# A decoder layer in fp32: the input projection in three passes over its rows in place of two, and heads four steps apart

## Chip, cores and metric

The kernel runs on one core of one Trainium2 chip. The metric is the device time of one execution in microseconds (us): the median of the runs.

## What is computed

```python
m = silu(c) @ w_mod + b_mod                     # 2048 -> 6 x 2048: sh1, sc1, g1, sh2, sc2, g2
hm = rms_norm(x) * (1 + sc1) + sh1              # x: 256 x 2048
q, k, v, o, g = split(hm @ w_in)                # 8 heads, q and k 128 wide, v and o 256 wide
y = (sigmoid(o) * rms_norm(mlstm(q, k, v, g)) * h_norm) @ w_out
x = x + g1 * y
hf = rms_norm(x) * (1 + sc2) + sh2
u = causal_conv3(hf @ w_up) + conv_b            # w_up: 2048 x 11264
x = x + g2 * ((silu(gate(u)) * val(u)) @ w_down)
```

All of it is fp32. Each product is computed as three products of fp32r parts (a rounded high part and the rest): high by high, high by low, low by high.

## The kernel before

**Shared stream of weights.** Weights come in as *halves* of 512 KB (`load_half` for `w_in`). For each half, ScalarE rounds it to `w_hi` (`split_hi`), VectorE subtracts to get `w_lo` (`split_lo`), and TensorE multiplies it (`in_half`, then `b_half`). `raw` holds eight halves, `w_hi` and `w_lo` four each. Step `p` of ScalarE and VectorE handles half `p + 3`, and ScalarE begins it when TensorE has finished `p` halves (`slot_hi`). So step `p` of these two engines lies beside TensorE's half `p`.

**Passes and strips.** The projection `hm @ w_in` needs scale and shift for the rows of `hm` that it multiplies. To begin before all of them are there, it is done in passes over the 16 row tiles (128 rows each). A pass goes through 12 *strips* of 512 columns (4 of V, 4 of O, 2 of K, 2 of Q), two row tiles a half. The first pass takes row tiles 0 to 5, the second 6 to 15. Between the passes a strip's sums are stored from PSUM to SBUF by ScalarE, and put back into PSUM (seeded) later. Strips of V and O take 12 matmuls of 512 columns a half, strips of K and Q 24 of 256.

**Scale and shift.** `m` is a vector: `w_mod` is read row tile by row tile. `load_m0` brings columns 0 to 767 of both chunks (scale, then shift) in 16 loads of two row tiles. VectorE adds three of four row tiles, scaled by `c`, to `acc` (`add_m0`), and TensorE sums the fourth and then the column sums of `acc` (`sum_m0`, `column_sums`). Columns 768 to 2047 follow during pass 1 (`load_m1`, `add_m1`, 32 loads of one row tile). The four other chunks are added in the same way later (`load_mod`, `add_mod`, 2048 columns at a time, called *accumulations* here), at steps that the table `MOD_SLOT` gives. Loads of the queue SP are issued in one order, written out by hand.

**Heads.** In the last pass V and O strips come last, and the eight heads of the mLSTM are worked off between the halves, in `attend(e)`, where `e` counts halves from the first V strip of that pass. TensorE's part of `attend(e)` stands behind half `e`; VectorE's part stands in step `e`, behind `split_lo` and ahead of the accumulation of that step. Head `h` has its scores behind half 5 + 5h (`E_SCORES`), its product with V behind 9 + 5h (`E_PV`), the gated output `gated` on VectorE in step 12 + 5h (`E_PV + 3`), and the transposes of `gated` behind half 13 + 5h (`E_HT`); `E_HEAD = 5` is the distance of two heads. TensorE runs its instructions in order, so the transposes, and every half behind them, wait for `gated`:

```python
h = head_at(e, E_HT)
if h is not None:
    pe.wait_ge(gated_made, 2 * h + 2)
```

Of the kernel before, what the change touches and what calls it, by code (L numbers as in the profile page):

```python
# [5 lines left out]
def hybrid_mlstm_convffn_adaln_kernel(nc, x_d, c_d, w_mod, b_mod, w_in, gate_bias, h_norm, w_out,  # L6
# [27 lines left out]
    K_FIRST = 6  # L34
    PAIRS = (K_FIRST // 2, (KT - K_FIRST) // 2)
    PASS = ([("V", j) for j in range(4)] + [("O", j) for j in range(4)]
            + [("K", 0), ("K", 1), ("Q", 0), ("Q", 1)],
            [("K", 0), ("K", 1), ("Q", 0), ("Q", 1)]
            + [(kind, j) for j in range(4) for kind in "VO"])
    STRIPS = len(PASS[0])  # L40
    V_PASS1 = STRIPS * PAIRS[0]
    V_VO = V_PASS1 + 4 * PAIRS[1]
    V_OUT = V_PASS1 + STRIPS * PAIRS[1]
# [5 lines left out]
    for n in CHUNKS:  # L49
# [13 lines left out]
    M0_COLS, M1_COLS = K_FIRST * P, (KT - K_FIRST) * P  # L63
    MODS_ALONE = 2 * KT


    MOD_SLOT = [V_PASS1 + p for p in (5, 7, 8, 10, 12, 13, 15, 17, 18)] \
        + [V_VO + e for e in (0, 1, 3, 4, 6, 8, 9, 11, 13, 14, 16, 18, 19, 21, 23, 24, 26, 28, 29, 31, 33, 34,
                              36, 38)] \
        + [V_OUT + f for f in (2, 4, 5, 7, 9, 10, 12, 13, 15, 17, 19, 21, 23, 26, 28)]  # L70
# [5 lines left out]
    MOD_LOAD = [V_PASS1 + 5, V_PASS1 + 6] + [max(V_PASS1 + 6, p + 11) for p in MOD_SLOT[:MOD_WIDE]] \  # L76
# [3 lines left out]
    E_SCORES, E_PV, E_HT, E_HEAD = 5, 9, 13, 5  # L80
    E_GATE = 18

    with ExitStack() as ctx:
# [12 lines left out]
        m0 = place("m0", [P, 8, 2 * M0_COLS], 0)  # L96
        m1 = place("m1", [P, 3, M1_COLS], 32 * KB)
# [95 lines left out]
        evac0, seeded, evac1 = sem("evac0"), sem("seeded"), sem("evac1")  # L193
# [112 lines left out]
        def _(sp):  # L306
# [24 lines left out]
            def load_m0(i):  # L331
                n, rows = i // 8, 2 * (i % 8) * P
                if i >= 8:
                    wait_m0(i - 8)
                sp.dma_start(m0[:, i % 8, :].rearrange("p (j n) -> p j n", j=2),
                             w_mod[rows:rows + 2 * P, MOD_ORDER[n]:MOD_ORDER[n] + M0_COLS]
                             .rearrange("(j p) n -> p j n", p=P)).then_inc(m0_in[i % 8], 16)

            def load_m1(i):
                n, rows = i // KT, (i % KT) * P  # L340
                if i < 3:
                    wait_m0((14, 14, 15)[i])
                else:
                    sp.wait_ge(m1_used, i - 2)
                col = MOD_ORDER[n] + M0_COLS
                sp.dma_start(m1[:, i % 3, :], w_mod[rows:rows + P, col:col + M1_COLS])\
                  .then_inc(m1_in[i % 3], 16)

            def load_half(vh):
# [29 lines left out]
            for vh in range(6):  # L379
                load_half(vh)  # L380
            for i in range(2 * KT):
                load_m1(i)
                load_half(6 + i)
            for vh in range(6 + 2 * KT, V_OUT):
# [59 lines left out]
        def _(pool):  # L444
# [83 lines left out]
            pool.wait_ge(colsum_done, 5)  # L528
# [20 lines left out]
        def _(act):  # L549
# [87 lines left out]
            def store_strip(m):  # L637
                for b in range(2):
                    nc.scalar.activation(strip_sums(0, m)[b], bank_pair(m, b), ACT.Copy)\
                             .then_inc(evac0, 1)  # L640

            def seed_strip(m):

                if m == STRIPS:
                    act.wait_ge(evac0, 2 * (STRIPS - 1))
                elif m == STRIPS + 1:
                    act.wait_ge(evac0, 2 * STRIPS)
                else:
                    act.wait_ge(evac1, 2 * (m - 1 - STRIPS))
                for b in range(2):  # L650
                    nc.scalar.activation(bank_pair(m, b), strip_sums(1, m)[b], ACT.Copy)\
                             .then_inc(seeded, 1)
# [897 lines left out]
```

## Time and profile before

| | |
|---|---|
| time, median of 3 runs | 1219.88 us (1215.63 to 1220.29) |
| span of the profiled execution | 1212.4 us |
| TensorE (PE) busy | 1187.3 us, 98% of the span |
| VectorE (DVE) busy | 922.2 us, 76% |
| ScalarE (ACT) busy | 623.4 us, 51% |
| bytes moved | 313.55 MB, mean 259 GB/s |

The profile gives its execution only by its span, from the first to the last instruction; it gives no time of its own for it. The runs lie 3.2 to 7.9 us above that span. What is worked out below is a difference of spans, and is taken off the median as it is.

How to read the rows: PE is TensorE's matmuls, PEld its weight loads, SPq the queue that issues the loads. PEclk is the granted clock of TensorE, where 1.00 is 2.4 GHz and 0.50 is 1.2 GHz. A busy PE is modelled to each matmul's end, so counts of matmuls in a stage say more than its share.

### The profile page before, as it was taken

How to read it: one execution, taken by the hardware profiler on the slowest of the kernel's cores; microseconds unless marked ns; L12 is line 12 of the kernel's file. 1: busy time of each engine (PE TensorE's matmuls, PEld its weight loads, DVE VectorE, ACT ScalarE, POOL GpSimd, SP SyncE). 2: the span in 40 equal slices, each digit the busy share in tenths (PEclk: the TensorE clock that was granted, in tenths of full speed). 3: DMA queues.
4: the chain of work that ended last, by engine and by line, in shares of the span. 5: the costliest groups of instructions: out<-in, count | busy, mean ns of one | idle time of the engine just before them, and what ended most of it. 6: DMA issues, size and time to landing. Idle time of an engine off the chain costs nothing.

```text
span 1212.4 us, 18009 instructions
## 1 busy us (share of the span) xinstructions
PE 1187.3 (98%) x6338; PEld 1020.6 (84%) x6338; DVE 922.2 (76%) x1016; ACT 623.4 (51%) x888; POOL 147.0 (12%) x158
## 2 busy tenths in 40 slices
PE   5899999999999999999999999999999999999998
PEld 5788999877788888888888888888888888888887
DVE  5899878788897897998887446888885446777654
ACT  4354564655554456565554445555554545555442
POOL 0000110001111120221121000212211000221100
PEclk9699999999999998999999999999999999999999
DMA  9999989798989994898885568878865566676542
GB/s 361 369 397 401 395 283 392 295 373 306 327 311 346 387 308 137 243 260 227 232 251 207 180 208 241 229 210 256 231 210 203 181 204 177 189 191 176 203 160 85
DMA packets 260028, 313.55 MB, mean 259 GB/s; under 512 B 6056, under 2 KB 186728, under 8 KB 251272
## 3 DMA queue, kind: packets, MB, share of 16 engines
q1 hardware_dynamic: 259360, 312.51, 78.0%
q8 instruction: 32, 0.52, 0.2%
q10 hardware_dynamic: 442, 0.21, 0.1%
q0 software_dynamic: 176, 0.16, 0.1%
q14 instruction: 18, 0.15, 0.0%
HBM read 310.76 MB, written 2.10 MB: 258 GB/s over the span
## 4 chain that ended last, share of the span: by engine, by line
PE 84%; DMA 8%; DVE 4%; issue 1%; SPq 1%; ACT 1%; DVEq 0%; ACTq 0%
PE ps L1203 27%; PE ps L1204 14%; PE ps L1231 9%; PE ps L1232 9%; PE ps L1233 9%; DMA m<-in_l_w_mod_dram 7%; PE ps L1280 2%; PE ps L1282 2%; PE ps L1281 2%; PE ps L1290 2%; PE ps L1293 2%; PE ps L1292 2%; DVE acc L905 1%; DVE acc L932 1%; PE ps L1301 1%
## 5 line engine op out<-in xcount | busy, mean ns | idle before, releaser
L892 DVE TENSOR_TENSOR w_lo<-raw,w_hi 128x1024 fp32r<-128x1024 f32 x392 | 481.9, 1231 | 197.8 <-ACT w_hi L559 197.1
L559 ACT ACTIVATE w_hi<-raw 128x1024 fp32r<-128x1024 f32 x392 | 414.1, 1057 | 357.9 <-PE ps L1233 167.7
L1203 PE MATMUL ps<-hm,w_hi 128*128 128x512 f32 x1408 | 495.9, 398 | 0.0
L1204 PE MATMUL ps<-hm,w_lo 128*128 128x256 f32 x1408 | 394.2, 280 | 0.0
L1203 PEld LDWEIGHTS ps<-hm,w_hi 128*128 128x128 f32 x1408 | 265.1, 188 | 65.5 <-issue 0.3
L1204 PEld LDWEIGHTS ps<-hm,w_lo 128*128 128x128 f32 x1408 | 266.1, 189 | 0.1
L1231 PE MATMUL ps<-w_hi,act_hi 128*128 128x512 f32 x344 | 134.3, 390 | 0.0
L1233 PE MATMUL ps<-w_hi,act_lo 128*128 128x512 f32 x344 | 133.9, 389 | 0.0
L1232 PE MATMUL ps<-w_lo,act_hi 128*128 128x512 f32 x344 | 133.9, 389 | 0.0
L1280 PE MATMUL ps<-w_hi,hm 128*128 128x512 f32 x256 | 103.6, 405 | 2.7 <-DVE hm L943 2.7
L1282 PE MATMUL ps<-w_hi,hm 128*128 128x512 f32 x256 | 100.4, 392 | 0.0
L539 POOL TENSOR_TENSOR act_full<-conv_gate,conv_val 128x256 f32<-128x256 f32 x44 | 32.5, 738 | 558.9 <-DVE conv_val L1173 558.9
L1281 PE MATMUL ps<-w_lo,hm 128*128 128x512 f32 x256 | 100.2, 391 | 0.0
L905 DVE SCALAR_TENSOR_TENSOR acc<-mod_raw,cT,acc 128x2048 f32<-128x2048 f32 x40 | 94.7, 2368 | 2.6 <-DMA mod_raw<-in_l_w_mod_dram 1.6
L853 ACT ACTIVATE up_sum<-ps 128x256 f32<-128x256 f32 x88 | 33.5, 380 | 106.5 <-PE ps L1204 106.5
L1231 PEld LDWEIGHTS ps<-w_hi,act_hi 128*128 128x128 f32 x344 | 64.6, 188 | 13.7 <-issue 0.2
L1233 PEld LDWEIGHTS ps<-w_hi,act_lo 128*128 128x128 f32 x344 | 64.6, 188 | 13.5
L1232 PEld LDWEIGHTS ps<-w_lo,act_hi 128*128 128x128 f32 x344 | 64.6, 188 | 13.4 <-issue 0.2
L1290 PE MATMUL ps<-hm,w_hi 128*128 128x256 f32 x256 | 73.3, 286 | 0.0
L1293 PE MATMUL ps<-hm,w_lo 128*128 128x256 f32 x256 | 73.2, 286 | 0.0
L1292 PE MATMUL ps<-hm,w_hi 128*128 128x256 f32 x256 | 73.1, 286 | 0.0
L543 POOL TENSOR_TENSOR act_lo<-act_full,act_hi 128x256 f32 x44 | 65.1, 1479 | 23.7 <-DVE act_hi L1180 23.7
(181 smaller groups left out, 1377.8 us busy)
## 6 DMA issues: line engine op xcount, KB each, us to landing
raw<-in_l_w_up_dram SPq DMA_DIRECT2D x88, 1024.0 KB, 5.9
mod_raw<-in_l_w_mod_dram SPq DMA_DIRECT2D x56, 1024.0 KB, 6.5
raw<-in_l_w_in_dram SPq DMA_DIRECT2D x96, 512.0 KB, 8.1
raw<-in_l_w_down_dram SPq DMA_DIRECT2D x44, 1024.0 KB, 5.0
m<-in_l_w_mod_dram SPq DMA_DIRECT2D x32, 640.0 KB, 7.2
raw<-in_l_w_out_dram SPq DMA_DIRECT2D x16, 1024.0 KB, 8.5
m<-in_l_w_mod_dram SPq DMA_DIRECT2D x16, 768.0 KB, 13.5
mod_wide<-in_l_w_mod_dram SPq DMA_DIRECT2D x8, 1024.0 KB, 7.2
```

Source lines behind the costliest of these rows:

```text
L559: nc.scalar.activation(w_hi[:, v % 4, :], raw[:, v // 2 % 4, (v % 2) * HALF:(v % 2 + 1) * HALF], ACT.Copy).then_inc(w_hi_made, 1)
L892: nc.vector.tensor_tensor(w_lo[:, v % 4, :], raw[:, v // 2 % 4, (v % 2) * HALF:(v % 2 + 1) * HALF], w_hi[:, v % 4, :].bitcast(f32), ALU.su ...
L905: nc.vector.scalar_tensor_tensor(out=part, in0=src, scalar=cT[:, ds(tile, 1)], in1=part, op0=ALU.mult, op1=ALU.add).then_inc(mod_done, 1)
L1203: mm(ps[:, 4 + w % 4, :], hi, both, start=(k == 0), stop=False, skip_group_check=True)
L1204: return mm(ps[:, 4 + w % 4, 0:SEQ], lo, hm_hi[:, k, :], start=False, stop=(k == KT - 1), skip_group_check=True)
L1231: mm(out, s_hi, hi, start=first, stop=False, skip_group_check=True)
L1232: mm(out, s_hi, lo, start=False, stop=False, skip_group_check=True)
L1233: last = mm(out, s_lo, hi, start=False, stop=final, skip_group_check=True)
L1280: mm(out, s_hi, hi, start=(k == 0), stop=False, skip_group_check=True)
L1281: mm(out, s_hi, lo, start=False, stop=False, skip_group_check=True)
L1282: last = mm(out, s_lo, hi, start=False, stop=(k == final), skip_group_check=True)
L1290: mm(out, hi, hm_hi[:, k, :], start=(k == 0 and f % 2 == 0), stop=False, skip_group_check=True)
```

## The change

- Three passes over row tiles: 0 to 3, 4 to 7, 8 to 15. Twelve strips more are stored and seeded.
- `load_m0` brings 512 columns of scale and shift, in 16 loads of 512 KB that have 16 buffers of their own.
- The other columns come in two groups: 512 columns in 16 loads of two row tiles for pass 2, and 1024 columns in 32 loads of one row tile for pass 3. They are added at steps 0 to 15 (two a step) and 16 to 43.
- The last pass has four halves a strip in place of five: 16 halves of K and Q and 32 of V and O, where there were 20 and 40. The number of halves in all stays 96.
- The heads stand four halves apart. `E_PV + 3` is still 12, and `E_HT` is now 12. The table of accumulations is new: ten in the K and Q steps (nine before), 21 in the 32 V and O steps (24 in 40), 17 behind them (15).

```diff
-    K_FIRST = 6
-    PAIRS = (K_FIRST // 2, (KT - K_FIRST) // 2)
+    K_AT = (0, 4, 8, KT)
+    LAST = len(K_AT) - 2
+    PAIRS = [(K_AT[n + 1] - K_AT[n]) // 2 for n in range(LAST + 1)]
...
-    MOD_SLOT = [V_PASS1 + p for p in (5, 7, 8, 10, 12, 13, 15, 17, 18)] \
...
+    M_TILES = (2, 1)
+    M_LOADS = [2 * KT // r for r in M_TILES]
+    M_FIRST = [0, M_LOADS[0]]
+    M_ADDS = [(n, i, j) for n in range(2) for i in range(M_LOADS[n]) for j in range(M_TILES[n])]
+    ADD_SLOT = [a // 2 for a in range(2 * KT)] + [KT + a * 28 // (2 * KT) for a in range(2 * KT)]
+    LOAD_HALF = [4 + i for i in range(M_LOADS[0])] + [4 + KT + i * 27 // (2 * KT) for i in range(M_LOADS[1])]
...
+    MOD_SLOT = [V_LAST + p for p in (3, 4, 6, 7, 8, 10, 11, 12, 14, 15)] \
+        + [V_VO + e for e in (0, 1, 3, 4, 6, 7, 9, 10, 12, 13, 15, 17, 18, 19, 21, 23, 24, 25, 27, 29, 30)] \
+        + [V_OUT + f for f in (1, 2, 3, 5, 6, 8, 9, 10, 11, 13, 15, 17, 19, 21, 23, 26, 28)]
...
-    E_SCORES, E_PV, E_HT, E_HEAD = 5, 9, 13, 5
-    E_GATE = 18
+    E_SCORES, E_PV, E_HT, E_HEAD = 5, 9, 12, 4
+    E_GATE = 16
...
-        m0 = place("m0", [P, 8, 2 * M0_COLS], 0)
-        m1 = place("m1", [P, 3, M1_COLS], 32 * KB)
+        m0 = place("m0", [P, 16, 2 * M0_COLS], 16 * KB)
+        m1 = place("m1", [P, 4, KB], 32 * KB)
...
-            for p in range(V_PASS1):
+            for p in range(V_VO):
                 in_half(p)
-                if p == 24:
-                    pe.wait_ge(m1_used, KT)
-                    pe.wait_ge(sc_made, 2)
-                    column_sums(0, SUM_BANK[0], K_FIRST, KT)
-                if p == V_PASS1 - 3:
-                    pe.wait_ge(m1_used, 2 * KT)
-                    column_sums(1, SUM_BANK[1], K_FIRST, KT)
-            for p in range(V_PASS1, V_VO):
-                in_half(p)
+                for n in range(1, LAST + 1):
+                    for chunk in range(2):
+                        if p == V_AT[n] - (9, 3)[chunk]:
+                            pe.wait_ge(m1_used, 2 * KT * (n - 1) + KT * (chunk + 1))
+                            pe.wait_ge(sc_made, 2 * n)
+                            column_sums(chunk, SUM_BANK[chunk], K_AT[n], K_AT[n + 1])
```

The change moves instructions at three places. The first is TensorE ahead of the first half: the sum of the last load and the column sums of the shift chunk. Before:

```order
L1337 MATMUL ps<-cT,m_51 128x1 [waits m0_in6]
L1337 MATMUL ps<-cT,m_51 128x1 x5
L1301 MATMUL ps<-ones,acc 128x1 [waits m0_used]
L1301 MATMUL ps<-ones,acc 128x1 x5
L1280 MATMUL ps<-w_hi,hm 128x512 [waits raw_done,hm_made]
```

and now:

```order
L1348 MATMUL ps<-cT,m_51 128x1 [waits m0_in14]
L1348 MATMUL ps<-cT,m_51 128x1 x3
L1312 MATMUL ps<-ones,acc 128x1 [waits m0_used]
L1312 MATMUL ps<-ones,acc 128x1 x3
L1291 MATMUL ps<-w_hi,hm 128x512 [waits raw_done,hm_made]
```

Six column tiles became four at each step, and the loads have semaphores (`m0_in`) of their own.

The second is VectorE at the head of pass 1, where `m_52` is the buffer of the later columns and `w_lo` is the split of a half. Before:

```order
L939 TENSOR_SCALAR hm_full<-hm_full,scale_p,shift_p 128x256
L943 TENSOR_TENSOR hm<-hm_full,hm 128x256
L892 TENSOR_TENSOR w_lo<-raw,w_hi 128x1024 x2
L932 SCALAR_TENSOR_TENSOR acc<-m_52,cT,acc 128x1280
L892 TENSOR_TENSOR w_lo<-raw,w_hi 128x1024
L932 SCALAR_TENSOR_TENSOR acc<-m_52,cT,acc 128x1280
```

and now:

```order
L964 TENSOR_TENSOR hm<-hm_full,hm 128x256
L897 TENSOR_TENSOR w_lo<-raw,w_hi 128x1024 x2
L939 SCALAR_TENSOR_TENSOR acc<-m_52,cT,acc 128x512 x2
L897 TENSOR_TENSOR w_lo<-raw,w_hi 128x1024
L939 SCALAR_TENSOR_TENSOR acc<-m_52,cT,acc 128x512 x2
L897 TENSOR_TENSOR w_lo<-raw,w_hi 128x1024
```

One addition of 1280 columns a step became two of 512; from step 16 on it is one of 1024 in most steps.

The third is VectorE at the heads, behind the first V strip of the last pass: the accumulation `acc<-mod_raw` ends a step, and `gated` is what TensorE's transposes wait for. One head before:

```order
L905 SCALAR_TENSOR_TENSOR acc<-mod_raw,cT,acc 128x2048
L892 TENSOR_TENSOR w_lo<-raw,w_hi 128x1024
L1021 SCALAR_TENSOR_TENSOR probs<-ps,weights 128x384
L1042 SCALAR_TENSOR_TENSOR gated<-ps,small,o_sig 128x256 x2
L892 TENSOR_TENSOR w_lo<-raw,w_hi 128x1024
L905 SCALAR_TENSOR_TENSOR acc<-mod_raw,cT,acc 128x2048
L892 TENSOR_TENSOR w_lo<-raw,w_hi 128x1024
L1002 TENSOR_SCALAR m_sel<-m_row,ident 8x256
```

and a head now:

```order
L910 SCALAR_TENSOR_TENSOR acc<-mod_raw,cT,acc 128x2048
L897 TENSOR_TENSOR w_lo<-raw,w_hi 128x1024
L1032 SCALAR_TENSOR_TENSOR probs<-ps,weights 128x384
L910 SCALAR_TENSOR_TENSOR acc<-mod_raw,cT,acc 128x2048
L897 TENSOR_TENSOR w_lo<-raw,w_hi 128x1024
L1013 TENSOR_SCALAR m_sel<-m_row,ident 8x256
L1053 SCALAR_TENSOR_TENSOR gated<-ps,small,o_sig 128x256 x2
L897 TENSOR_TENSOR w_lo<-raw,w_hi 128x1024
```

`gated` moved from the step of `probs` to the next one. It stands behind one accumulation, one split and `m_sel` more. On TensorE the transposes stand one half nearer to the product with V: behind the half that lies beside the step of `gated`, where before they stood behind the half after it.

## Rows read from the trace of the kernel before

**Rows 1.** The page: span, and busy time of each engine.

```profile
span 1212.4 us, 18009 instructions
...
PE 1187.3 (98%) x6338; PEld 1020.6 (84%) x6338; DVE 922.2 (76%) x1016; ACT 623.4 (51%) x888; POOL 147.0 (12%) x158
```

**Rows 2.** Busy time by stage; last columns: granted clock, DMA share, GB/s.

```profile
core 0: us, PE busy (x) PEld busy (x) DVE busy (x) ACT busy (x) POOL busy (x), PEclk, DMA share, GB/s
28.00:41.86 13.86, 12.14 (x58) 11.97 (x58) 10.18 (x11) 0.00 (x0) 0.00 (x0) 0.52 1.03 399
...
60.00:100.00 40.00, 40.00 (x178) 33.15 (x177) 37.79 (x29) 20.07 (x25) 0.00 (x0) 1.00 1.03 398
147.66:158.00 10.34, 10.34 (x75) 10.34 (x76) 7.06 (x11) 4.99 (x10) 3.49 (x3) 0.83 0.96 342
176.00:214.80 38.80, 38.80 (x325) 38.80 (x325) 33.80 (x22) 17.81 (x21) 0.00 (x0) 1.00 0.97 369
265.00:339.20 74.20, 73.17 (x335) 58.26 (x336) 65.65 (x83) 41.62 (x71) 10.41 (x16) 1.00 0.89 318
```

**Rows 3.** Timeline up to the first projection matmul: start, length, engine, line.

```profile
41.86 2.07 DVE L923 SCALAR_TENSOR_TENSOR acc<-m,cT,acc 128x768 f32<-128x768 f32 x2 [0.74 <-DMA m<-in_l_w_mod_dram]
...
43.99 2.72 PE L1301 MATMUL ps<-ones,acc 128*128 128x1 f32 x12 [1.36 <-DVE acc L923]
...
44.57 1.06 ACT L559 ACTIVATE w_hi<-raw 128x1024 fp32r<-128x1024 f32 x1 [0.30 <-DMA raw<-in_l_w_in_dram]
...
46.95 2.08 ACT L597 ACTIVATE hm<-hm_full,shift_p,scale_p 128x256 fp32r<-128x256 f32 x4
...
49.40 0.80 PE L1280 MATMUL ps<-w_hi,hm 128*128 128x512 f32 x1 [2.69 <-DVE hm L943]
```

**Rows 4.** Waits, TensorE alone: total us, times, longest.

```profile
PE ps L1393 <- DVE gated L1042: 1.1, 2, 0.7
PE ps L1301 <- DVE acc L932: 0.3, 1, 0.3
```

**Rows 5.** The page's DMA issues: KB each, median us to landing.

```profile
mod_raw<-in_l_w_mod_dram SPq DMA_DIRECT2D x56, 1024.0 KB, 6.5
...
m<-in_l_w_mod_dram SPq DMA_DIRECT2D x16, 768.0 KB, 13.5
```

**Rows 6.** Timeline, TensorE, the later column sums of the shift chunk.

```profile
147.66 2.39 PE L1301 MATMUL ps<-ones,acc 128*128 128x1 f32 x20 [0.28 <-DVE acc L932]
```

**Rows 7.** Lines from 49.4 to 214.8 us: count, busy us, mean ns.

```profile
L892 DVE TENSOR_TENSOR w_lo<-raw,w_hi 128x1024 fp32r<-128x1024 f32 x56 | 68.4, 1221 | 8.9 <-ACT w_hi L559 8.6
...
L932 DVE SCALAR_TENSOR_TENSOR acc<-m,cT,acc 128x1280 f32<-128x1280 f32 x32 | 49.6, 1550 | 6.3 <-DMA m<-in_l_w_mod_dram 6.0
```

**Rows 8.** Timeline of one head on TensorE, VectorE and ScalarE (others left out).

```profile
320.76 0.60 PE L1393 MATMUL ps<-ident,gated 128*128 128x128 f32 x4
...
324.60 0.33 DVE L1002 TENSOR_SCALAR m_sel<-m_row,ident 8x256 f32<-8x256 f32 x1
...
333.60 2.34 DVE L905 SCALAR_TENSOR_TENSOR acc<-mod_raw,cT,acc 128x2048 f32<-128x2048 f32 x1
...
333.75 0.39 PE L1280 MATMUL ps<-w_hi,hm 128*128 128x512 f32 x1
...
335.86 1.22 DVE L892 TENSOR_TENSOR w_lo<-raw,w_hi 128x1024 fp32r<-128x1024 f32 x1
...
336.47 0.39 PE L1280 MATMUL ps<-w_hi,hm 128*128 128x512 f32 x1
...
336.67 1.06 ACT L559 ACTIVATE w_hi<-raw 128x1024 fp32r<-128x1024 f32 x1 [1.48 <-PE ps L1282]
...
336.99 0.55 DVE L1021 SCALAR_TENSOR_TENSOR probs<-ps,weights 128x384 f32<-128x384 f32 x1
...
337.46 0.86 DVE L1042 SCALAR_TENSOR_TENSOR gated<-ps,small,o_sig 128x256 f32<-128x256 f32 x2
...
338.24 1.21 DVE L892 TENSOR_TENSOR w_lo<-raw,w_hi 128x1024 fp32r<-128x1024 f32 x1
```

More of the change, by code:

```diff
@@ L183, in hybrid_mlstm_convffn_adaln_kernel @@
         pool_step = sem("pool_step")
-        m0_in = [sem(f"m0_in{s}") for s in range(8)]
+        m0_in = [sem(f"m0_in{s}") for s in range(16)]
         m0_used, m0_summed = sem("m0_used"), sem("m0_summed")
-        m1_in = [sem(f"m1_in{s}") for s in range(3)]
+        m1_in = [sem(f"m1_in{s}") for s in range(4)]
         m1_used = sem("m1_used")
@@ L192, in hybrid_mlstm_convffn_adaln_kernel @@
         half_done = sem("half_done")
-        evac0, seeded, evac1 = sem("evac0"), sem("seeded"), sem("evac1")
+        stored, seeded = sem("stored"), sem("seeded")
         mod_in = [sem(f"mod_in{s}") for s in range(2)]
@@ L378, in _ @@
                 load_m0(i)
[L379 to L384, printed above, removed]
+            for vh in range(V_OUT):
+                for i in range(len(LOAD_HALF)):
+                    if LOAD_HALF[i] == vh:
+                        load_m1(i)
                 load_due_mods(vh)
@@ L635, in scale_shift, with seed_strip @@
                     nc.scalar.activation(out, src, ACT.Copy).then_inc(sc_made, 1)
-            def store_strip(m):
+            def seed_strip(m):
+                act.wait_ge(stored, 2 * (m - 1))
                 for b in range(2):
[L639 to L651, printed above, removed]
+                    nc.scalar.activation(bank_pair(m, b), strip_sums(m)[b], ACT.Copy)\
                              .then_inc(seeded, 1)
@@ L957, in _ @@
             dve.wait_ge(sc_made, 2)
-            dve.wait_ge(xT_copied, K_FIRST // 2)
-            for g in range(K_FIRST // 2):
+            dve.wait_ge(xT_copied, K_AT[1] // 2)
+            for g in range(K_AT[1] // 2):
                 modulate_lo(0, 2 * g, 2 * g + 2)
@@ L1260, in in_half @@
                 bank = strip_banks(m)
-                first, final = (0, 2 * PAIRS[0] - 1) if n == 0 else (2 * PAIRS[0], KT - 1)
+                first, final = K_AT[n], K_AT[n + 1] - 1
                 if 2 * kp == first and m >= 2:
                     if n == 0:
-                        pe.wait_ge(evac0, 2 * (m - 1))
+                        pe.wait_ge(stored, 2 * (m - 1))
                     else:
@@ L1334, in sum_m0 @@
                 n, rt = i // 8, 2 * (i % 8)
-                pe.wait_ge(m0_in[i % 8], 16 * (n + 1))
-                for k in range(K_FIRST):
-                    last = mm(ps[:, SUM_BANK[n], k:k + 1], m0[:, i % 8, k * P:(k + 1) * P],
+                pe.wait_ge(m0_in[i], 16)
+                for k in range(K_AT[1]):
+                    last = mm(ps[:, SUM_BANK[n], k:k + 1], m0[:, i, k * P:(k + 1) * P],
                               cT[:, rt:rt + 1], start=(rt == 0 and k == 0), stop=False,
@@ L1416, in attend @@
                     if h == 0:
-                        pe.wait_ge(evac1, 8)
+                        pe.wait_ge(stored, taken(4))
                         pe.wait_ge(aem_made, 1)
```

205 lines of the change are left out of this document (104 added, 101 removed).

## Prediction

> **What bounds the kernel now.** I read the page first: TensorE is busy for 98% of the span, VectorE for 76%, ScalarE for 51% [rows 1]. So the question is where TensorE waits, and what stands ahead of its first half. The waits of TensorE alone answer the first part: behind the start there are only 1.1 us for `gated` at two heads and 0.3 us for an addition ahead of the column sums [rows 4]. The timeline of the start answers the second. The last load of scale and shift is added from 41.86 us, the column sums end at 46.7, and the first half begins at 49.40 [rows 3]. In the stages until then the DMA engines are full, at 399 GB/s [rows 2]: the start is a matter of bytes, all that comes behind it of TensorE's instructions. The change leaves the projection's matmuls as they are. A V or O half lasts 2.70 us (178 matmuls in 40 us, 12 a half), a K or Q half 2.87 (325 in 38.8 us, 24 a half) [rows 2].
>
> **The start.** The 16 first loads shrink from 768 KB [rows 5] to 512 KB: 16 x 0.262 MB = 4.19 MB less, at 399 GB/s 10.5 us. Behind the last load two additions get shorter. One of 768 columns takes 1.03 us [rows 3], one of 1280 takes 1.55 [rows 7], so 1.0 ns a column, and 0.77 us at 512: 0.5 us less for two. The column sums are 8 records in place of 12, 2.72 / 12 each [rows 3]: 0.9 us less. Not all of this 1.4 us counts. The splits of the first two halves hang on loads that land behind the last of scale and shift, and ScalarE's second one ends at 45.63, 1.3 us ahead of the modulation at 46.95 [rows 3]; VectorE's splits follow. I take 0.8. The first half begins 11.3 us earlier. Bounds: TensorE also does 32 transposes and the sums of the loads ahead of this; with loads coming every 1.3 us in place of 2, I take at worst 1.5 us of that as backlog, so 9.8. At best the first halves no longer meet the half clock that the start leaves behind (0.50 to 0.52 until 49.4 [rows 2]); the first matmul takes 0.80 us where later ones take 0.39 [rows 3, 8], and some 3 us at half rate give 1.5 back: 12.8.
>
> The Trainium skill, "DMA: Bandwidth & Descriptors", section "Bandwidth", advises transfers of 1 MiB and more, and its section "Anatomy of one DMA — SWDGE (gpsimd) path" fits, for loads that GpSimd issues, 2.0 us + bytes / 436 GB/s to one of them. By that fit smaller pieces save less: 16 x 0.262 MB / 436 GB/s = 9.6 us, an estimate, and the fixed part stays. The trace agrees only in part: halves of 512 KB and pieces of 640 KB together move at 398 GB/s from 60 to 100 us [rows 2], so nothing of a fixed part shows where they queue.
>
> **Passes 1 and 2.** Twelve strips more are stored and seeded, four copies each on ScalarE, which is busy for half of the time [rows 1]; TensorE has two bank pairs, and a strip of two halves (5.4 us) covers split, store and seed. I cost it at nothing; were a strip late, it would show as a wait for `seeded`. VectorE has 1.22 + 2 x 0.77 = 2.76 us a step where it had 1.22 + 1.55 = 2.77 [rows 7]: the same. The DMA queue carries 48 pieces and 43 halves of 0.524 MB in 43 steps, 1.11 MB or 2.77 us a step at 400 GB/s; before it was 1.18 MB, 2.95 us, with 0.3 us of wait at its end [rows 4]. So nothing is added.
>
> Column sums: 24 tiles in place of 20, at 2.39 us for ten [rows 6], so 1.0 us more. But they are now four pieces of 1 to 1.9 us. Behind the old piece of 2.39 us the clock was granted at 0.83 over 10.3 us [rows 2, 6], worth 1.8 us. If shorter pieces leave it alone, the sum is 1.0 - 1.8 = -0.8 us. If the two of 1.9 us do what the one did, it is +2.8.
>
> **K and Q steps of the last pass.** Sixteen halves and ten accumulations of 1.05 MB are 18.9 MB, 47 us at 400 GB/s, against 16 x 2.87 = 45.9 us; before, 20 halves and nine made 19.9 MB in 57.4 us. An accumulation needs its buffer back: landing takes 6.5 us [rows 5] and the addition 2.3 [rows 8], with two buffers one in 4.4 us, and the table asks for one in 3.8. VectorE falls behind by 9 x 0.6 = 5 us at most. It works three halves (8.6 us) ahead, so I take 0, and 5 us as the upper bound.
>
> **The heads.** This is the price. `gated` and the transposes behind the same half now have one step between them less. Put T for the start of half 12 + 4h. ScalarE begins its split 0.20 us after a half starts (336.67 against 336.47) and takes 1.06; then VectorE's split 1.13 (335.86 to 336.99), `m_sel` 0.26 and `gated` 0.78 (337.46 to 338.24) [rows 8]. That ends at T + 3.43, while the half has ended at T + 2.72: TensorE waits 0.71 us in every head, even when VectorE is idle ahead of it. (`m_sel` is 0.33 long; 0.26 is from its start to the next one's.)
>
> Where the step before has an accumulation, the chain is longer. From the start of that step: 0.20 + 1.06 + 1.13, `probs` 0.47, the accumulation 2.26 (333.60 to 335.86), then 1.13 + 0.26 + 0.78, in all 7.29 us, against two halves of 2.72 [rows 8]: a wait of 1.85 us. A second look gives the same: the old head has `gated` done at 338.24, and its transposes due one half after 336.47, at 339.19, so 0.95 us early. One half less, and `m_sel` ahead of it, makes 2.0 us late. The table has an accumulation in steps 15, 19, 23, 27 and 35, and none in 11, 31 and 39. So five heads wait 1.85 and three 0.71: 11.4 us. What TensorE lost there before, 1.1 us [rows 4], goes off: +10.3. Queued behind the transposes is all of TensorE's stream, so nothing gives it back. Bounds: eight times the floor, 5.7 - 1.1 = 4.6; and above, 2.3 us a head if landings make accumulations late besides, 18.4 - 1.1 = 17.3.
>
> Is VectorE itself full? It was busy for 65.65 of 74.2 us over four heads, 16.4 a head, with five splits and three accumulations [rows 2]. With four and 2.6 it is 16.4 - 1.2 - 0.9 = 14.3, against 18.5 - 2.7 = 15.8 for TensorE. So it is the order, not the load.
>
> **Sum.** -11.3 - 0.8 + 0 + 10.3 = -1.8 us, on the profiled span of 1212.4 [rows 1] and so on the median: 1219.9 - 1.8 = 1218.
>
> **Rivals.**
> - *The heads wait less than I think (faster).* If accumulations don't delay `gated`, only the floor is left: -11.3 - 0.8 + 4.6 = -7.5, 1212 us. For it: VectorE has 1.5 us a head to spare. Against: the split, the accumulation and `gated` stand in one queue in this order. 0.2.
> - *The clock falls at the heads (slower).* Until now TensorE keeps 1.00 over the heads, with waits of 0.7 us [rows 2, 4]; it fell behind 0.28 us of wait and 2.39 us of column sums [rows 2, 6]. A wait of 1.85 us with transposes behind it comes near that. Each fall costs about 1.5 us, five of them 7.5: 1226. It decides from four falls on. 0.15.
> - *Late accumulations in the K and Q steps, and on into the first heads (slower).* Up to 5 us there and some 3 at the heads: 1226. For it: the queue is asked for 18.9 MB in the time of 18.4. 0.13.
> - *The change doesn't bring its start.* The bytes of scale and shift are the same in all, only later. If the queue were the bound up to the last piece, TensorE would wait there. Before, the column sums at 147.66 waited for the last addition of 1.55 us [rows 6, 7], so the last piece was there at 146 us. Ten halves more are due by the new last piece, 5.2 MB or 13 us: 159 us, where TensorE comes to its column sums at 38.1 + 1.5 + 124 + 2 = 166. Seven us are to spare; used up, they would cost about as much again, 1224. 0.07.
> - What I forecast: 0.45.
>
> The Trainium skill, "TensorE: Matmul & The Clock Gate", section "HAM oscillation — how this bites in real kernels", says that pauses between bursts of matmuls can put the array back to half rate, and that each one is then paid again. By that rule the heads would come out as in the second rival, 1226. In the trace so far the pauses of the heads leave the clock at 1.00 [rows 2, 4]; no row has one of 1.85 us.
>
> **How the numbers follow.** A measurement of this kernel tells about 0.5% (6 us) from no change. The forecast's own range adds its bounds in part: 1218 - 3 to 1218 + 5. The range reaches down to the first rival with the best start (1.5 us more), 1210, and up to the slow rivals with 3 us of the heads' upper bound, 1229. Faster than 1213.8: the first rival for the most part, and the forecast with a better start, 0.22. Slower than 1226: more than half of the slow rivals, and the forecast with the heads' upper bound, 0.26. Same: 0.52.
>
> **What the changed profile would show.** The first half at about 38.1 us; TensorE's waits with a line for `gated`, eight times, 11 us in all, of 0.7 and 1.9 us; column sums without a wait for additions; granted clock 1.00 over the heads. I am wrong if the waits for `gated` sum to under 6 us or over 16, if the clock falls there, or if waits for `raw_done` or `seeded` (splits of VectorE, seeds of ScalarE) show in passes 2 and 3.

## The result and the profile after

The changed kernel takes 1233.39 us (median of 4 runs, 1229.18 to 1236.14), the kernel before 1219.85 beside it: a ratio of 1.012, 95% interval 1.0098 to 1.0141. It is slower by 13.5 us where I forecast 1.8 us less, and outside my range. The profiled span went from 1212.4 to 1230.2 us, by 17.8. (A run of the changed kernel lies 1.8 us over its own span, 1232.01 against 1230.2; the profiled execution of before was one of its shorter ones.) One of the runs reported below, of e5, took 6658 us and is left out of the ratios.

The page of the changed kernel, as in [rows 1]:

```profile
span 1230.2 us, 18084 instructions
...
PE 1184.0 (96%) x6306; PEld 1015.1 (83%) x6306; DVE 931.1 (76%) x1048; ACT 650.1 (53%) x938; POOL 155.6 (13%) x158
```

TensorE's busy share fell from 98 to 96%. Its waits answer to [rows 4]: engine and line, what it waited for, us in all, times, longest. Those of the start are left out.

```profile
PE ps L1401 <- DVE gated L1053: 14.3, 8, 3.4
...
PE ps L1392 <- ACT em_row L732: 3.3, 1, 3.3
...
PE ps L1291 <- ACT ps L654: 3.0, 2, 1.8
...
PE ps L1301 <- ACT ps L654: 2.1, 1, 2.1
```

L1393 of before is L1401 now. Before, 1.4 us were waited behind the start; now it is 22.9, of which 0.2 for `hm` are not shown and the rest is in three groups. The first line is the heads. The second is `em_row`, a row of gate values that TensorE transposes at `e` = 3, ahead of the first head. The last two are matmuls that wait for a *seeded* bank pair (L654 is `seed_strip`, L1291 and L1301 are the first matmul of a V or O and of a K or Q strip). `gated` I had in the sum, `em_row` only in a rival, and the seeds at nothing.

Where the time goes by milestones, in us from the start of the span, read from TensorE's timeline:

| kernel | first half | K, Q of last pass from | V, O from | output projection from | column sums of chunk 3 |
|---|---|---|---|---|---|
| before | 49.4 | – | 220.5 | 362.7 | 400.0 |
| after | 38.7 | 185.6 | 237.3 | 371.4 | 417.7 |

Chunk 3, counted from 0 in `MOD_ORDER`, is `sc2`, and its column sums stand in the output projection. Behind them both kernels take the same, 812.4 and 812.5 us, so all of the 17.8 us lies ahead. From the first half to there the changed kernel takes 28.4 us longer (379.0 against 350.6): 21.5 more of waits (22.9 - 1.4), 1.0 of four more column tiles, about 4.4 of half clock (5.9 against 1.5, worked out below), and some 1.5 that no row names.

### The profile page after: what moved, and what is told of

The parts are those of the page before. It is cut to its first block, busy times and chain, and to the rows that moved or that the text cites. A ratio compares the mean times of both kernels' runs of the same rounds, so it can differ in the third digit from the quotient of the medians.

```text
span 1230.2 us, 18084 instructions
## 1 busy us (share of the span) xinstructions
PE 1184.0 (96%) x6306; PEld 1015.1 (83%) x6306; DVE 931.1 (76%) x1048; ACT 650.1 (53%) x938; POOL 155.6 (13%) x158
## 4 chain that ended last, share of the span: by engine, by line
PE 78%; DMA 8%; DVE 7%; issue 2%; ACT 2%; SPq 2%; POOL 1%; DVEq 0%; ACTq 0%; POOLq 0%
PE ps L1214 26%; PE ps L1215 13%; PE ps L1243 8%; PE ps L1242 8%; PE ps L1244 8%; DMA mod_raw<-in_l_w_mod_dram 5%; DMA raw<-in_l_w_in_dram 3%; PE ps L1291 2%; DVE acc L910 2%; PE ps L1292 2%; PE ps L1293 2%; SPq L347 2%; DVE w_lo L897 1%; ACT w_hi L572 1%; DVE acc L939 1%
## 5 line engine op out<-in xcount | busy, mean ns | idle before, releaser
L1291 PE MATMUL ps<-w_hi,hm 128*128 128x512 f32 x256 | 105.2, 411 | 6.2 <-DVE hm L964 3.2
L910 DVE SCALAR_TENSOR_TENSOR acc<-mod_raw,cT,acc 128x2048 f32<-128x2048 f32 x40 | 94.9, 2371 | 13.3 <-DMA mod_raw<-in_l_w_mod_dram 10.2
L1293 PE MATMUL ps<-w_hi,hm 128*128 128x512 f32 x256 | 101.4, 396 | 0.0
L1243 PEld LDWEIGHTS ps<-w_lo,act_hi 128*128 128x128 f32 x344 | 64.6, 188 | 13.5 <-issue 0.2
L1301 PE MATMUL ps<-hm,w_hi 128*128 128x256 f32 x256 | 72.8, 285 | 2.3 <-ACT ps L654 2.1
```

The lines of the kernel that those rows point to most:

```text
L910: nc.vector.scalar_tensor_tensor(out=part, in0=src, scalar=cT[:, ds(tile, 1)], in1=part, op0=ALU.mult, op1=ALU.add).then_inc(mod_done, 1)
L1243: mm(out, s_hi, lo, start=False, stop=False, skip_group_check=True)
L1291: mm(out, s_hi, hi, start=(k == 0), stop=False, skip_group_check=True)
L1293: last = mm(out, s_lo, hi, start=False, stop=(k == final), skip_group_check=True)
L1301: mm(out, hi, hm_hi[:, k, :], start=(k == 0 and f % 2 == 0), stop=False, skip_group_check=True)
```

## Experiments

Eleven kernels, each an edit of the changed kernel, timed against the kernel before. Ratios have their 95% interval. The last column is the milestone of above, where TensorE comes to the column sums of chunk 3: 400.0 us before and 417.7 in the changed kernel.

| run | median us | ratio | span | waits for `gated`, us, times | column sums at |
|---|---|---|---|---|---|
| e1 | 1228.1 | 1.0084 (1.0053 to 1.0115) | 1226.7 | 8.3, 6 | 411.0 |
| e2 | 1235.85 | 1.0149 (1.0117 to 1.0181) | 1234.9 | 15.2, 8 | 419.3 |
| e3 | 1225.33 | 1.0067 (1.0042 to 1.0092) | 1218.3 | 6.6, 8 | 407.1 |
| e4 | 1235.25 | 1.0155 (1.0121 to 1.0189) | 1228.6 | 13.3, 8 | 415.7 |
| e5 | 1220.46 | 1.003 (1.0009 to 1.0051) | 1219.4 | 3.5, 5 | 402.0 |
| e6 | 1228.21 | 1.0095 (1.0069 to 1.0122) | 1225.1 | 15.4, 8 | 412.5 |
| e7 | 1230.87 | 1.0121 (1.0085 to 1.0157) | 1226.3 | 14.2, 8 | 413.8 |
| e8 | 1218.82 | 0.9999 (0.9982 to 1.0015) | 1218.2 | 5.5, 5 | 402.1 |
| e9 | 1210.23 | 0.9933 (0.9914 to 0.9953) | 1207.3 | 5.8, 6 | 394.4 |
| e10 | 1214.27 | 0.9975 (0.9957 to 0.9993) | 1210.8 | 4.5, 5 | 398.1 |
| e11 | 1236.42 | 1.0136 (1.0111 to 1.0161) | 1235.8 | 15.0, 8 | 419.7 |

The spans need care. Behind the milestone the edits move nothing but a few accumulations, and yet five kernels take 815.6 to 817.4 us there (e1, e2, e5, e8, e11) and the others 811.2 to 812.9. From 80 to 200 us behind it, TensorE issues 339 to 342 matmuls in 60 us in the five and 345 to 348 in the others, at a granted clock of 1.00 in all. No run shows why. So what an edit does to the passes and the heads is read at the milestone, and a span carries up to 6 us of something else.

### The heads: e1 and e3

e1 puts `gated` at the head of its step:

```diff
+                gate_head(p - V_VO)          # the lines of `gated`, taken out of attend
                 split_lo(p + 3)
                 attend(p - V_VO)
```

> Changed kernel, but VectorE computes gated at the head of its step, ahead of split_lo and m_sel; nothing else moves. Order theory: the transposes wait because gated stands behind a split that hangs on ScalarE (1.26 us after the half begins) and its own 1.13 us. Without it the chain from the accumulation of the step before ends 0.4 us behind the half and without that accumulation ahead of it: TensorE's waits for gated fall from 14.3 us to 3 or 4, and the two falls of the clock over the heads go too (0.91 in 320 to 340 and 380 to 400, 1.8 us each): span 1230.2 to about 1216. Load theory (rival): VectorE is simply full over the heads, so it falls behind elsewhere and TensorE waits for raw_done instead: span within 3 us of 1230.

e3 takes the accumulations out of the steps ahead of `gated`:

```diff
-        + [V_VO + e for e in (0, 1, 3, 4, 6, 7, 9, 10, 12, 13, 15, 17, 18, 19, 21, 23, 24, 25, 27, 29, 30)] \
-        + [V_OUT + f for f in (1, 2, 3, 5, 6, 8, ...
+        + [V_VO + e for e in (0, 1, 3, 4, 6, 7, 9, 10, 12, 13, 16, 17, 18, 20, 21, 22, 24, 25, 26, 28, 29)] \
+        + [V_OUT + f for f in (1, 2, 4, 5, 6, 8, ...
```

> Changed kernel with another table: no accumulation in the steps just ahead of gated (15, 19, 23, 27, 35 moved to steps 16, 20, 22, 26 and 36 and their neighbours); the same number of accumulations. By the prediction's chain five heads fall from 1.9 us or more to the floor of 0.7, so the waits for gated from 14.3 to about 6, and the clock's falls with them: span 8 to 11 us less (1221). Load theory: the accumulations only gather elsewhere, within 3 us.

TensorE's timeline at the transposes, first the changed kernel; in brackets what was waited:

```profile
286.45 0.66 PE L1401 MATMUL ps<-ident,gated 128*128 128x128 f32 x4 [1.41 <-DVE gated L1053]
303.55 0.66 PE L1401 MATMUL ps<-ident,gated 128*128 128x128 f32 x4 [2.17 <-DVE gated L1053]
...
321.58 0.66 PE L1401 MATMUL ps<-ident,gated 128*128 128x128 f32 x4 [2.28 <-DVE gated L1053]
340.87 0.66 PE L1401 MATMUL ps<-ident,gated 128*128 128x128 f32 x4 [1.87 <-DVE gated L1053]
358.50 0.66 PE L1401 MATMUL ps<-ident,gated 128*128 128x128 f32 x4 [1.87 <-DVE gated L1053]
...
393.37 0.66 PE L1401 MATMUL ps<-ident,gated 128*128 128x128 f32 x4 [3.44 <-DVE gated L1053]
```

and e3:

```profile
302.11 0.66 PE L1401 MATMUL ps<-ident,gated 128*128 128x128 f32 x4 [0.73 <-DVE gated L1053]
318.62 0.66 PE L1401 MATMUL ps<-ident,gated 128*128 128x128 f32 x4 [0.73 <-DVE gated L1053]
335.14 0.65 PE L1401 MATMUL ps<-ident,gated 128*128 128x128 f32 x4 [0.73 <-DVE gated L1053]
```

The two numbers of the prediction stand there: 1.85 us behind a step with an accumulation was 1.87, and the floor of 0.71 was 0.73. Without accumulations ahead of it, five heads are at the floor, and the column sums of chunk 3 come 10.6 us earlier: 7.7 us of waits, and the clock falls behind them. (The span is 11.9 us shorter, but the profiled execution was the shortest of six; by the ratios, 1.0067 against 1.012, it is some 6.5 us.) e1 takes away the floor and leaves what lies ahead: 6.0 us less of waits, where I expected 10 or more, and the column sums 6.7 us earlier. What I had too small is heads 0, 1 and 2 by 0.3 to 0.7 us each and above all head 6, with 3.44. At head 0, VectorE stands idle for 0.58 us until GpSimd has made `o_sig`, an operand of `gated`. VectorE's timeline ahead of head 6, in the changed kernel:

```profile
383.13 2.35 DVE L910 SCALAR_TENSOR_TENSOR acc<-mod_raw,cT,acc 128x2048 f32<-128x2048 f32 x1
385.62 1.26 DVE L897 TENSOR_TENSOR w_lo<-raw,w_hi 128x1024 fp32r<-128x1024 f32 x1
386.81 0.54 DVE L1032 SCALAR_TENSOR_TENSOR probs<-ps,weights 128x384 f32<-128x384 f32 x1
389.04 2.35 DVE L910 SCALAR_TENSOR_TENSOR acc<-mod_raw,cT,acc 128x2048 f32<-128x2048 f32 x1 [1.69 <-issue]
391.31 1.22 DVE L897 TENSOR_TENSOR w_lo<-raw,w_hi 128x1024 fp32r<-128x1024 f32 x1
392.44 0.87 DVE L1053 SCALAR_TENSOR_TENSOR gated<-ps,small,o_sig 128x256 f32<-128x256 f32 x2
```

VectorE stands idle for 1.69 us ahead of the accumulation at 389.04, and `gated` is behind it. The timeline names no releaser for this idle time, but the landings do. SP issued the load for this accumulation at 379.80, when the one of 377.37 had given its buffer back, and it took 9.2 us to land: 389.0. The median before was 6.5 [rows 5]; the DMA engines were full here, at 396 GB/s from 378 to 390 us. (The load issued at 385.57 is for the accumulation after this one.) In e3, with no accumulation in that step, this head waits 0.48 us.

### The first two passes: e2, e6 and e7

e2 takes and seeds a strip ahead of the split in its step on ScalarE. e6 brings only half of the bytes of the loads for pass 3 and leaves out the rest of these columns. e7 leaves all the bytes and moves these loads behind three more halves in the queue:

```diff
-            for p in range(V_VO):
-                slot_hi(p)
-                take_before(p)
+            for p in range(V_VO):                                  # e2
+                wait_from_1(act, half_done, p)
+                take_before(p)
+                split_hi(p + 3)
...
+                if g == 1:                                         # e6
+                    sp.dma_start(m1[:, i % 4, 0:cols // 2],
+                                 w_mod[tile * P:(tile + 1) * P, col:col + cols // 2])...
...
-    LOAD_HALF = ... + [4 + KT + i * 27 // (2 * KT) for i in range(M_LOADS[1])]
+    LOAD_HALF = ... + [7 + KT + i * 27 // (2 * KT) for i in range(M_LOADS[1])]    # e7
```

> Changed kernel, but at the start of a strip in passes 1 and 2 and the K and Q steps ScalarE stores the last strip and seeds the next one ahead of its split, not behind it. Order theory: TensorE's 5.1 us of waits for seeded PSUM come from the copies standing behind a split that waits for a late half (ScalarE waits 20 us for halves from 120 to 175 us), not from missing weights, since three split halves lie ready: the waits for seeding go, span 5 to 7 us less (1224). Supply theory (rival): the halves are late anyway, TensorE waits for raw_done in their place, span within 2 us.

> Leaves out half of the bytes of the loads for pass 3 (512 of 1024 columns are brought, the additions still go over 1024, so scale and shift are wrong there): 8.4 MB, 21 us of the DMA queue between 85 and 165 us. Theory A (the bytes are short in passes 1 and 2): the waits of 5.1 us for seeded banks go, K and Q of the last pass begin at 178 to 180 us where the changed kernel has 185.6, span down by 6 us or more. Rival B (the order of the queue: a load waits for the additions of VectorE, which is modulating from 103 to 109 us, and halves wait behind it): the gap of the queue at 103.5 to 109.5 stays, and K and Q begin at 184 or later.

> The loads for pass 3 stand three halves later in the queue; same bytes, same additions. Theory B (order of the queue): halves are issued up to three steps earlier against the additions, the gap of 6 us in the queue at 103.5 no longer holds a half back, waits for seeded banks fall from 5.1 us to under 2, K and Q of the last pass begin at 178 to 181 us, span down by about 5 us to 1225. Theory A (bytes): no change there, 185 us; or the column sums of shift wait for a late last addition.

Start with the changed kernel's queue, SP's timeline at the boundary of passes 1 and 2 (L360 is `load_m1`, L372 `load_half`):

```profile
103.16 0.33 SPq L360 DMA_DIRECT2D m<-in_l_w_mod_dram  x1
103.53 0.43 SPq L372 DMA_DIRECT2D raw<-in_l_w_in_dram  x1
109.46 0.33 SPq L360 DMA_DIRECT2D m<-in_l_w_mod_dram  x1
109.83 0.43 SPq L372 DMA_DIRECT2D raw<-in_l_w_in_dram  x1
```

For 5.5 us nothing is issued. `load_m1` waits for an addition of VectorE, which modulates row tiles 4 to 7 in those steps, and the half stands behind it. What that does to the DMA engines and to TensorE is in the busy times by stage (columns as in [rows 2]). The changed kernel, then e7:

```profile
100.00:120.00 20.00, 19.79 (x166) 19.59 (x165) 17.08 (x21) 14.30 (x24) 0.00 (x0) 1.00 0.84 279
...
124.00:182.00 58.00, 52.91 (x281) 44.98 (x281) 46.88 (x39) 40.92 (x63) 4.29 (x3) 1.00 1.00 359
```

```profile
100.00:120.00 20.00, 19.79 (x165) 19.59 (x165) 17.07 (x21) 14.89 (x26) 0.00 (x0) 1.00 0.96 343
...
124.00:182.00 58.00, 58.00 (x316) 50.38 (x315) 49.17 (x46) 43.03 (x66) 6.04 (x5) 1.00 1.01 381
```

The gap of VectorE's making is in both; but in e7 halves are ahead of it, and the engines move 343 GB/s over the boundary in place of 279. From 124 to 182 us TensorE issues 316 matmuls in place of 281 and is never idle. Who waited shows in the groups by line from 120 to 182 us, ScalarE's split (its last field is the idle time ahead of it and what ended that), first the changed kernel, then e7:

```profile
L572 ACT ACTIVATE w_hi<-raw 128x1024 fp32r<-128x1024 f32 x20 | 21.1, 1055 | 21.3 <-DMA raw<-in_l_w_in_dram 20.3 <-PE ps L1293 1.0
```

```profile
L572 ACT ACTIVATE w_hi<-raw 128x1024 fp32r<-128x1024 f32 x22 | 23.2, 1055 | 16.2 <-PE ps L1293 11.3 <-PE ps L1304 4.8
```

In the changed kernel the split waits for its half 20.3 us in all, and the seeds, which stand behind the split on ScalarE, are late with it. In e7 it waits only for TensorE. K and Q of the last pass begin at 181.2 us in place of 185.6, and the waits for seeds are gone. In e6, with half of the bytes, they begin at 180.8, though the gap stays, 5.5 us as before. My expectation for e6 had set the two theories apart wrongly (I wrote that only the byte theory would bring 180): fewer bytes also let the queue catch up behind the gap. It is e7, at the full bytes, that decides: they can be moved in time if nothing holds the halves back. e2 leaves the halves late and only lets the seed go first: seed waits 5.1 to 1.8 us, but K and Q begin only 1.4 us earlier, the heads are later, and no time is gained. The seeds were where it showed, not its cause.

At the column sums of chunk 3 e7 is 3.9 us ahead of the changed kernel, where I expected 5. In the median it can't be told from nothing (1.0121 against 1.012). In pairs it can: e10 is e5 with it, 0.9975 against 1.003, and e9 is e8 with it, 0.9933 against 0.9999.

### The end of the K and Q steps: e4, e5, e8, e9, e10

e4 moves the accumulation of step `e` = 0 to `e` = 2, e5 is e1 and e3 together, e8 has eight accumulations in the K and Q steps in place of ten and none at `e` = 0 and 1. e9 and e10 are e8 and e5 with the loads of e7. The table of e8 and e9:

```diff
-    MOD_SLOT = [V_LAST + p for p in (3, 4, 6, 7, 8, 10, 11, 12, 14, 15)] \
-        + [V_VO + e for e in (0, 1, 3, 4, 6, 7, 9, 10, 12, 13, 15, 17, 18, 19, 21, 23, 24, 25, 27, 29, 30)] \
-        + [V_OUT + f for f in (1, 2, 3, 5, 6, 8, 9, 10, 11, 13, 15, 17, 19, 21, 23, 26, 28)]
+    MOD_SLOT = [V_LAST + p for p in (3, 4, 6, 7, 9, 10, 12, 13)] \
+        + [V_VO + e for e in (2, 3, 4, 6, 7, 9, 10, 12, 13, 14, 16, 17, 18, 20, 21, 22, 24, 25, 26, 28, 29)] \
+        + [V_OUT + f for f in (1, 2, 4, 5, 6, 8, 9, 10, 11, 12, 13, 15, 17, 19, 21, 23, 25, 26, 28)]
```

> Changed kernel with the accumulation of step 0 of the V and O halves moved to step 2. Late-accumulation theory: the scans of step 1 stand behind it on VectorE (it began at 245.5 after a DMA wait of 1.8 us), em_row and TensorE's transposes behind half 3 behind the scans: without it the wait of 3.3 us for em_row goes, and with it the half at half clock (0.83 from 240 to 260 us): span 4 to 6 us less (1225). Rival: ScalarE's table loads and the gate projection set the scans, which then begin no earlier; within 1 us.

> Gated ahead of the split and m_sel in its step, and no accumulation in the step ahead of gated. Theory A (the loss at the heads is VectorE's order alone): the floor of 0.71 us goes too, waits for gated under 2 us in all where the changed kernel has 14.3 and e3 alone 6.6; the span falls from e3's 1218.3 by some 5 us to 1213, median near 1220. Rival B (VectorE is full, or the accumulations that were moved behind the heads cost there): waits of over 5 us stay or come up in the output projection, span 1218 or more.

> As e5, and eight accumulations in the K and Q steps in place of ten, none in the first two steps behind them (they go to later steps, none of them ahead of gated). Theory (accumulations asked for faster than two buffers bring them make VectorE late, so the scans, em_row and m_sel are late): no wait of TensorE for em_row (3.3 us) or m_sel at 250 us, granted clock 1.00 in 240 to 260 us where it was 0.83, span 5 us under e5. Rival (the clock falls there anyway from the small matmuls of the gates, or the moved accumulations make gated late again): clock under 0.95, or waits for gated up by 3 us; span as e5.

> e8 (gated first in its step, accumulations off the step ahead of gated and fewer in the K and Q steps) with the loads for pass 3 three halves later, as in e7. If the causes add, the 4.4 us that e7 gains at the beginning of K and Q come on top of e8: K and Q of the last pass from 182 us, span 1218.2 - 4 = 1214, the median at 0.997 of the kernel before, so the change is mended but gains next to nothing over before. Rival: what comes earlier there is lost at the heads (waits for gated over 6 us) or in a clock fall, and the span stays at 1218.

> e5 with the loads for pass 3 three halves later: ten accumulations in the K and Q steps as in the changed kernel. If late accumulations in those steps still matter, the wait for em_row (2.4 us in e5) stays or grows towards 4.0 as in e7, and the span is 1 to 3 us over e9. If they do not, it is equal to e9, near 1214 to 1215.

VectorE of the changed kernel ahead of `em_row`:

```profile
240.30 2.35 DVE L910 SCALAR_TENSOR_TENSOR acc<-mod_raw,cT,acc 128x2048 f32<-128x2048 f32 x1 [1.13 <-DMA mod_raw<-in_l_w_mod_dram]
242.57 1.22 DVE L897 TENSOR_TENSOR w_lo<-raw,w_hi 128x1024 fp32r<-128x1024 f32 x1
245.54 2.35 DVE L910 SCALAR_TENSOR_TENSOR acc<-mod_raw,cT,acc 128x2048 f32<-128x2048 f32 x1 [1.75 <-DMA mod_raw<-in_l_w_mod_dram]
247.81 1.22 DVE L897 TENSOR_TENSOR w_lo<-raw,w_hi 128x1024 fp32r<-128x1024 f32 x1
248.94 0.67 DVE L998 TENSOR_TENSOR_SCAN neg_b<-ones_row,neg_lf 8x256 f32<-8x256 f32 x1
```

Two accumulations wait for their bytes, and the scans of `e` = 1, from which `em_row` is made, come behind them at 248.94, where TensorE needs the result soon after. And TensorE's timeline behind that wait:

```profile
251.73 1.02 PE L1392 MATMUL ps<-ident,a_row 8*128 8x8 f32 x4 [3.34 <-ACT em_row L732]
252.60 1.00 PE L1392 MATMUL ps<-ident,em_row 8*128 8x8 f32 x4
253.53 0.80 PE L1291 MATMUL ps<-w_hi,hm 128*128 128x512 f32 x1
254.12 0.63 PE L1292 MATMUL ps<-w_lo,hm 128*128 128x512 f32 x1
...
257.54 0.42 PE L1291 MATMUL ps<-w_hi,hm 128*128 128x512 f32 x1
```

The matmuls take 0.63 us each where they take 0.39 at full clock [rows 8]: half clock, nine matmuls long. These nine took 4.01 us (253.53 to 257.54), at full clock 9 x 2.70 / 12 = 2.0. The transposes ahead of them, 1.80 us, are slow too. In e5 the same wait, 2.4 us there, has no fall behind it, and from the first transposes to the start of the tenth matmul it is 3.16 us where the changed kernel takes 5.81: this fall costs 2.7 us behind its wait.

In e4 the wait for `em_row` is gone, and the same lateness shows one matmul group later:

```profile
258.34 1.19 PE L1432 MATMUL ps<-m_sel,ones 8*128 8x256 f32 x2 [3.10 <-DVE m_sel L1013]
```

So moving one accumulation by two steps only moved the wait: the milestone is 2.0 us earlier, and the median no better than that of the changed kernel (ratio 1.0155).

e5 puts e1 and e3 together, and its column sums come 15.7 us earlier than in the changed kernel, though 5 us of that don't show in its span. I expected under 2 us of waits for `gated`, and there are 3.5. Behind the mended order another engine shows that I had left out. VectorE of e8, at the first two heads:

```profile
282.11 0.88 DVE L1000 SCALAR_TENSOR_TENSOR gated<-ps,small,o_sig 128x256 f32<-128x256 f32 x2 [1.08 <-POOL o_sig L517]
...
298.28 0.88 DVE L1000 SCALAR_TENSOR_TENSOR gated<-ps,small,o_sig 128x256 f32<-128x256 f32 x2 [1.04 <-POOL small L515]
```

Both operands are made by GpSimd (POOL): L515 is the scale of the head, `h_scale`, L517 the sigmoid of `o`. VectorE waits for them 5.7 us in all in e5, 7.8 in e8 and 7.7 in e9. No run moves GpSimd's part, so what it is worth stays open.

e8 took two accumulations out of the K and Q steps and kept them off `e` = 0 and 1, and neither wait is left but 0.7 us of `m_sel`; which of the two did it was not tried apart. Against e5 nothing was gained that can be told, where I expected 5 us: column sums at 402.1 and 402.0, and ratios whose intervals overlap. The first head waits for `gated` in both (2.57 and 2.21 us), but in e8 the waits for `gated` are 2.0 us more in all, and seven matmuls at half clock stand behind the first. With the queue mended as well, e9 against e10 shows it: e10 waits 3.5 us for `em_row`, e9 does not, column sums at 394.4 against 398.1, spans 1207.3 against 1210.8, ratios 0.9933 against 0.9975 with intervals that lie apart. All waits of TensorE behind the start in e9 are these:

```profile
PE ps L1405 <- DVE gated L1000: 5.8, 6, 2.0
...
PE ps L1436 <- issue: 0.3, 1, 0.3
PE ps L1490 <- DVE rstd_diag L1134: 0.3, 1, 0.3
PE ps L1305 <- DVE hm L964: 0.2, 1, 0.2
```

e9 is faster than the kernel before by 0.67% (0.47 to 0.86). Its milestones are 38.8, 180.0, 231.7, 353.6 and 394.4: the start's gain of 10.6 us is still 5.6 at the column sums of chunk 3 and 5.1 in the span. So the change can pay, once the seed waits and the wait for `em_row` are gone and those for `gated` are cut from 14.3 to 5.8 us.

### The rate at the start: e11

```diff
-                sp.dma_start(m0[:, i, :].rearrange("p (j n) -> p j n", j=2),
-                             w_mod[rows:rows + 2 * P, MOD_ORDER[n]:MOD_ORDER[n] + M0_COLS]...
+                sp.dma_start(m0[:, i, :], w_mod[rows:rows + P, MOD_ORDER[n]:MOD_ORDER[n] + 2 * M0_COLS])...
```

e11 brings one row tile of 1024 columns in each load where the changed kernel brings two row tiles of 512: the same bytes, but rows of 4 KB, and half of the row tiles that the sum needs are left out.

> Each of the 16 first loads brings one row tile of 1024 columns in place of two row tiles of 512 (the values are wrong for scale and shift, the bytes and the instructions of all engines the same): rows of 4 KB in place of 2 KB. Theory (the length of a row sets the rate): the DMA engines move 399 to 401 GB/s from 20 to 36 us where the changed kernel has 386 to 387, and the first half begins 0.5 us earlier, at 38.2. Rival (the number of loads or something else of the start sets it): 386 GB/s and 38.7 us as before. The whole time: the same as the changed kernel within 0.2%.

Busy times by stage, 10 to 36 us, the changed kernel and then e11; the last column is GB/s:

```profile
10.00:36.00 26.00, 19.12 (x116) 18.45 (x116) 19.55 (x27) 14.35 (x21) 1.32 (x2) 0.86 1.05 387
```

```profile
10.00:36.00 26.00, 21.43 (x116) 21.33 (x116) 19.09 (x26) 14.29 (x18) 0.95 (x2) 0.83 1.03 400
```

The rate follows the rows: 387 GB/s with rows of 2 KB, 400 with 4 KB, and 399 in the kernel before with 3 KB [rows 2], the DMA engines being full each time (share over 1). The first half did not come earlier, though: 39.15 us against 38.71. The last additions begin at 32.50 in place of 32.05, behind a wait of 1.50 us for their load. Over all kernels with the new start it lies between 38.66 and 39.19, so half a microsecond is not to be told there, and what the rate is worth in time stays open.

## Why the prediction was wrong

- **The start, -11.3 us: right.** The first half came 10.7 us earlier. The 0.6 us that are missing would fit a rate of 387 GB/s in place of the 399 that I took over from longer rows, but e11 had 400 and did not bring them; their cause is open.
- **"So nothing is added" in passes 1 and 2: this step failed.** 5.1 us of waits for seeds, and K and Q of the last pass at 185.6 us where my own durations give 178.2 (38.7, 132.3 for 32 V and O and 16 K and Q halves, 5.7 of column sums, 1.5 of half clock). I compared sums, bytes and VectorE's time per step with the time of a half, and both fitted. I did not ask what each load waits for in the queue, and I left VectorE's modulation at the new boundary out of the sum: for 5.5 us the queue issues nothing. e7, which changes only the order of issue, brings 4.4 of these 7.4 us back, and e9 and e10, with the same queue, 5.6. The rest stands in no row of waits.
- **K and Q steps, "I take 0": right for these steps, wrong for what follows.** TensorE does not wait from 185.6 to 231.7 us. But VectorE leaves them late. I had named the pace (an accumulation in 4.4 us, asked for one in 3.8), and had trusted the lead of three halves. The lead ends at the scans of `e` = 1, which have none: 3.3 us of wait, and a fall of the clock. e4 shows that it is VectorE's lateness and not the scans' place; e8 and e9 show that it goes with fewer accumulations there and none at `e` = 0 and 1.
- **The heads, 11.4 us of waits: mechanism right, size 2.9 us too small.** 14.3 us in eight waits, and the two sizes were met (1.87 and 0.73). What was missing is in heads 0, 1, 2 and 6. In head 6 it is the upper bound's "landings make accumulations late besides": a load that landed after 9.2 us, and VectorE idle for 1.69 us. In head 0 it is mostly GpSimd's `o_sig`, 0.58 us, which is in no term of mine. In head 2 `m_sel` took 0.70 us in place of 0.33, and for head 1 it is open.
- **The column sums, -0.8 us: right in direction.** The four short pieces leave the clock at 1.00 between 80 and 182 us. The old fall behind the piece of 2.39 us [rows 2] is gone, but others came.
- **The rival "the clock falls at the heads": came in part.** In the changed kernel the granted clock is 0.83 in 240 to 260 us and 0.91 in 320 to 340 and 380 to 400. The first cost 2.7 us (above). The second cost 1.6: from the transposes at 321.58 to the next group of matmuls behind the half it is 5.74 us, and 4.09 at the head of 340.87, which had no fall. The third cost 1.6 too: 4.84 us from 393.37 on, and 3.25 in e3's last head. That is 5.9 us, against 1.5 that before lost in its own fall (16 K and Q matmuls in 3.40 us, where a half of 24 takes 2.87); in the sum I had taken 1.8 for that one. The rule of the Trainium skill, "TensorE: Matmul & The Clock Gate", section "HAM oscillation — how this bites in real kernels", that a pause brings the array back to half rate and that each one is then paid again, holds here for the longer waits; most of the short ones leave the clock alone (counts below). My "each fall costs about 1.5 us" holds for two of the three, and my limit for this rival, four falls, was not reached.

In all I forecast -1.8 us of span and 17.8 came. The error of 19.6 is made of 0.6 of the start, 7.4 of passes 1 and 2, 3.3 for `em_row`, 2.9 of the heads and 5.9 of the clock, of which I had taken none. (Together that is 20.1; half a microsecond is counted twice or saved elsewhere.) No term alone does it. The two largest waits that I had put at nothing, those of the passes and of `em_row`, are one mistake: I costed each engine's sum of work and not the queue in which a late item holds the next one.

## What to carry to other kernels

When loads for two consumers share one queue in order, look up for every load what it waits for: one that waits for an engine with a burst of other work ahead holds back all behind it, though bytes and busy times fit on average. Put such loads behind those that can go at once. A lead of some steps hides late work only as far as the next operation without a lead; find that one. And before a change is dropped, take away its waits one by one: here three edits of order turned 1.2% slower into 0.7% faster.

## What the runs showed of the hardware

Rows of 2 KB in the memory moved at 387 GB/s and rows of 4 KB at 400, at 512 KB a load in both and with the DMA engines full. The Trainium skill, "DMA: Bandwidth & Descriptors", section "Bandwidth", goes by the size of a transfer, which was the same in both; the difference here is that of the rows. And the longer a wait, the more often the clock fell. Behind all 17 waits of 2.94 us and more that stand behind the start, in the changed kernel and the eleven of the experiments, 5 to 12 of TensorE's next matmuls of 512 columns ran at half rate. Behind eight waits of 2.28 to 2.57 us that was so six times, and behind some 70 waits of 0.6 to 2.21 us four times (1.54, twice 1.87, and 1.98 us). The wait of 3.34 us cost 6.0 in this way. It isn't the wait alone: before and in e9 the rate also falls ahead of or behind the column sums of chunk 3 with no wait of such a length.
